# Expert row gathers issued as buffers free, the emptier expert moved to a y bank, rounded slot products: a decoder step with 64 experts on one NeuronCore

## The reference, cut to what matters

```python
def moe_ffn(h, lw):
    x = h.reshape(-1, h.shape[-1])                      # 1032 x 1024
    idx, wts = route(x, lw['router_w'], lw['router_bias'])   # 8 of 64 experts per token
    routed = routed_experts(x, idx, wts, lw['expert_w_gate'], lw['expert_w_up'], lw['expert_w_down'])
    shared = (silu(x @ lw['shared_w_gate']) * (x @ lw['shared_w_up'])) @ lw['shared_w_down']
    return routed + shared
# per expert e and the tokens that chose it (gate and up 1024 x 256, down 256 x 1024):
#   hb = silu(xb @ w_gate[e]) * (xb @ w_up[e]);  out[token] += (hb @ w_down[e]) * weight[token, e]
```

## Time and profile before

| what | before |
|---|---|
| median of three runs | 1831.04 us |
| the profiled execution: its time, and its span | 1831.6 us, 1829.8 us |
| PE / weight loads / DVE / ACT / GpSimd busy | 90% / 65% / 62% / 49% / 34% of the span |
| granted TensorE clock, mean | 0.953 of full |
| stages by time | to 748 us attention and mixing; 748 to 841 routing; 841 to 1752 experts; to 1830 the rest |
| share of DMA xg<-h_d,tokb in the chain that ended last | 22.0%, the largest |

### The profile page before, as it was taken

How to read it: one execution, slowest core, us unless ns; L and a number is a source line. 1 busy time by engine, 2 the same in 40 slices (tenths; PEclk the granted TensorE clock), 3 DMA queues, 4 the chain that set the end, 5 groups by cost and what they waited for, 6 DMA issues and landing times.

```text
span 1829.8 us, 26568 instructions
## 1 busy us (share of the span) xinstructions
PE 1643.9 (90%) x8857; PEld 1187.0 (65%) x8858; DVE 1129.6 (62%) x1575; ACT 904.9 (49%) x1389; POOL 626.5 (34%) x555
## 2 busy tenths in 40 slices
PE   4999999599998898687999999999999899999897
PEld 3555555333356667366888888878888787787743
DVE  2355575532235556666778777777787777777746
ACT  1011111232345454135777776776776676676633
POOL 0056676300000000113543554545455354454300
PEclk8999999689999999798999999999999999999999
DMA  9588866667761113646989889888898898988774
GB/s 349 195 279 274 273 207 216 246 205 217 238 226 63 65 52 152 255 156 244 311 287 316 294 300 319 277 301 304 281 328 283 295 312 279 329 278 299 267 240 187
DMA packets 156011, 457.45 MB, mean 250 GB/s; under 512 B 25375, under 2 KB 35806, under 8 KB 138458
## 3 DMA queue, kind: packets, MB, share of 16 engines
q1 hardware_dynamic: 119289, 368.12, 55.7%
q0 software_dynamic: 26624, 69.80, 14.7%
q10 hardware_dynamic: 9960, 17.83, 2.8%
HBM read 394.52 MB, written 78.15 MB: 258 GB/s over the span
## 4 chain that ended last, share of the span: by engine, by line
PE 28%; DMA 22%; issue 4%; ACT 2%; POOLq 1%; DVE 1%; POOL 1%; ACTq 0%; DVEq 0%
DMA xg<-h_d,tokb 22%; PE ps L2341 10%; PE ps L2360 6%; PE ps L2303 4%; PE ps L2694 2%; ACT yb L2266 2%; PE ps L2323 2%; PE ps L1840 1%; PE ps L1885 1%; PE ps L2712 1%; PE ps L2325 1%; PE ps L1856 1%; POOLq L2167 1%; POOL acc_d L2176 1%; PE ps L2328 0%
## 5 line engine op out<-in xcount | busy, mean ns | idle before, releaser
L2395 DVE TENSOR_TENSOR lo_gu<-raw_gu,hi_gu 128x1024 fp32r<-128x1024 f32 x256 | 301.5, 1219 | 14.5 <-ACT hi_gu L2216 13.1
L2176 POOL DMA_INDIRECT acc_d<-yb,tokb x96 | 175.6, 1829 | 344.5 <-ACT yb L2266 324.1
L2323 PE MATMUL ps<-xT_h,hi_gu 128*128 128x416 f32 (+4 forms) x896 | 266.1, 361 | 1.4 <-DVE gu_h L2409 1.4
L2216 ACT ACTIVATE hi_gu<-raw_gu 128x1024 fp32r<-128x1024 f32 x256 | 255.3, 1049 | 0.0
L602 PE MATMUL ps<-w_in_sb,hT 128*128 128x512 f32 x512 | 225.4, 598 | 1.1 <-ACT hT L466 1.1
L2325 PE MATMUL ps<-xT_h,lo_gu 128*128 128x208 f32 (+4 forms) x896 | 224.7, 251 | 0.0
L446 POOL TENSOR_TENSOR prod<-kring,qbc 128x512 f32<-128x512 f32 x128 | 159.5, 1274 | 177.6 <-DMA kring<-in_cache_k 122.2
L602 PEld LDWEIGHTS ps<-w_in_sb,hT 128*128 128x128 f32 x512 | 96.5, 191 | 118.7 <-issue 117.4
L2323 PEld LDWEIGHTS ps<-xT_h,hi_gu 128*128 128x128 f32 x896 | 169.1, 189 | 5.0 <-issue 2.4
L2325 PEld LDWEIGHTS ps<-xT_h,lo_gu 128*128 128x128 f32 x896 | 171.3, 191 | 1.2
L2360 PE MATMUL ps<-hi_dn,hT_h 128*128 128x512 f32 (+5 forms) x512 | 168.5, 400 | 0.0
(11 more groups left out here) (362 smaller groups left out, 2979.6 us busy)
## 6 DMA issues: line engine op xcount, KB each, us to landing
raw_gu<-in_expert_w_gate SPq DMA_DIRECT2D x64, 1024.0 KB, 9.9
raw_gu<-in_expert_w_up SPq DMA_DIRECT2D x64, 1024.0 KB, 13.5
raw_dn<-in_expert_w_down SPq DMA_DIRECT2D x64, 1024.0 KB, 10.0
kring<-in_cache_k SPq DMA_DIRECT2D x128, 256.0 KB, 3.1
vring<-in_cache_v SPq DMA_DIRECT2D x128, 256.0 KB, 3.0
adaw<-in_ada_w ACTq DMA_DIRECT2D x7, 2048.0 KB, 12.7
adaw<-in_ada_w SPq DMA_DIRECT2D x5, 2048.0 KB, 15.2
w_in_sb<-in_w_in SPq DMA_DIRECT2D x4, 2048.0 KB, 19.5
```

What stands on the lines that cost most here:

```text
L2176: pool.indirect_dma_start(out=acc_d[b % 2][:, :], out_offset=bass.IndirectOffsetOnAxis(ap=tokb[0:rows, b:b + 1], axis=0), in_=yb[b % 2][0: ...
L2216: act.activation(hi_cut(n, u), raw_cut(n, u), ACT.Copy).then_inc(hi_made, 1)
L2323: pe.matmul(ps[:, bank, 0:2 * cap], wh, x[:, k, :, :].rearrange("p a t -> p (a t)"), start=(k == 0), stop=False)
L2395: dve.tensor_tensor(lo_cut(n, u), raw_cut(n, u), hi_cut(n, u).bitcast(F32), ALU.subtract).then_inc(lo_made, 1)
```

## The change

Six things are done together.

1. GpSimd's order is written out by pair: gathers 0 to 3 ahead of the wait for the cleared accumulators, then scatter(3p-2), gather(3p+4), slot_weight(3p+2), scatter(3p-1), gather(3p+5), slot_weight(3p+3), gather(3p+6), slot_weight(3p+4), scatter(3p). The wslot ring grows from 4 to 6.
2. The light block's turn_x(3p+2) moves from the head of the pair into heavy ch 0, between its two halves; ACT and DVE handle it after the first three weight cuts instead of before them.
3. The light gate/up writes the first y bank of block 3p+1's parity (light_bank) instead of gate_bank. Its wait for sums_h 2p+2 becomes a wait for y_here 3p and moves, itself, to turn_h.
4. down(3p+1) writes that y bank next and gets a wait for hb_made p+1.
5. The slot products (L1885) take fp32r operands instead of fp32; they and ACT's numbered are spread between the steps of the shared expert, and turn_down(2) goes ahead of the last four.
6. The waits for y5_out go from GpSimd, ahead of gather(2), to ACT's first second_halves and DVE's rest_of_x(2).

```diff
         OH = 3
-        oh_p = [place(f"oh_p{j}", 160 + 4 * j, [P, TOPK, P]) for j in range(OH)]
-        oh_b = [place(f"oh_b{j}", 172 + 5 * j, [P, TOPK, NBLK]) for j in range(OH)]
+        oh_p = [place(f"oh_p{j}", 160 + 4 * j, [P, TOPK, P], F32R) for j in range(OH)]
+        oh_b = [place(f"oh_b{j}", 172 + 5 * j, [P, TOPK, NBLK], F32R) for j in range(OH)]
         y5 = [place(f"y5_{j}", dead + 4 * j, [P, D]) for j in range(2)]
...
                 act.wait_ge(oh_b_made, t + 1)
-                act.activation(oh_b[t % OH][:, :, :], oh_b[t % OH][:, :, :], ACT.Copy,
+                act.activation(oh_b[t % OH][:, :, :], oh_b[t % OH][:, :, :].bitcast(F32), ACT.Copy,
                                scale=c("ids")[:, t:t + 1]).then_inc(oh_b_ids, 1)
...
             evict(0)
+            numbered(0)
+            numbered(1)
             gated(2)
+            numbered(2)
             turned(1)
+            numbered(3)
+            numbered(4)
             evict(1)
-            for t in range(T9):
-                numbered(t)
+            numbered(5)
             turned(2)
+            numbered(6)
+            numbered(7)
             evict(2)
+            numbered(8)
             act.wait_ge(zeros_out, 16 * (2 * T9 - NWIN))
...
                 last.then_inc(dn5, 1)
...
+            def slots_of(t):
+                pe.wait_ge(oh_p_made, t + 1)
+                pe.wait_ge(oh_b_ids, t + 1)
+                for k in range(TOPK):
+                    last = pe.matmul(ps[:, 0, 0:NBLK], oh_p[t % OH][:, k, :], oh_b[t % OH][:, k, 0:NBLK],
+                                     start=(t == 0 and k == 0), stop=(t == T9 - 1 and k == TOPK - 1))
+                last.then_inc(tok_mm, 1)
 
...
             gate_up(2)
+            slots_of(0)
+            slots_of(1)
+            slots_of(2)
             turn_down(1)
-            for t in range(T9):
-                pe.wait_ge(oh_p_made, t + 1)
-                pe.wait_ge(oh_b_ids, t + 1)
-                for k in range(TOPK):
-                    last = pe.matmul(ps[:, 0, 0:NBLK], oh_p[t % OH][:, k, :], oh_b[t % OH][:, k, 0:NBLK],
-                                     start=(t == 0 and k == 0), stop=(t == T9 - 1 and k == TOPK - 1))
-                last.then_inc(tok_mm, 1)
+            slots_of(3)
+            slots_of(4)
+            turn_down(2)
+            for t in range(5, T9):
+                slots_of(t)
             pe.wait_ge(over_made, 1)
...
                       ).then_inc(over_mm, 1)
-            turn_down(2)
 
...
         wr = [place(f"wr{j}", 206 + 0.25 * j, [P, NE]) for j in range(4)]
-        wslot = [place(f"wslot{j}", 207 + j / 32, [P, 1]) for j in range(4)]
+        wslot = [place(f"wslot{j}", 207 + j / 32, [P, 1]) for j in range(6)]
         s_gu2 = place("s_gu2", 89, [P, 2, KC * F])
...
             return 2 + p % 2
...
+        def light_bank(p):
...
+            return 4 + 2 * ((3 * p + 1) % 2)
 
...
                 pool.wait_ge(wr_in[b % 4], 16 * (b // 4) + 16)
-                if b >= 4:
-                    pool.wait_ge(y_here, b - 3)
-                pool.tensor_copy(wslot[b % 4][:, :], wr[b % 4][:, bass.ds(e, 1)]).then_inc(wslot_here, 1)
+                if b >= 6:
+                    pool.wait_ge(y_here, b - 5)
+                pool.tensor_copy(wslot[b % 6][:, :], wr[b % 4][:, bass.ds(e, 1)]).then_inc(wslot_here, 1)
 
...
             pool.wait_ge(tok_ready, 1)
-            gather(0)
-            gather(1)
+            for b in range(4):
+                gather(b)
             pool.wait_ge(zeros_out, 16 * (2 * T9 - NWIN))
...
                 pool.wait_ge(y5_out[j], 16 * ((NWIN + 1 - j) // 2))
-            for b in range(MAIN):
-                if b + 2 < MAIN:
-                    gather(b + 2)
-                slot_weight(b)
-                if b >= 3:
-                    scatter(b - 3)
-            for b in range(MAIN - 3, MAIN):
-                scatter(b)
+            slot_weight(0)
+            slot_weight(1)
+            for p in range(PAIRS):
+                if p:
+                    scatter(3 * p - 2)
+                if p + 1 < PAIRS:
+                    gather(3 * p + 4)
+                slot_weight(3 * p + 2)
+                if p:
+                    scatter(3 * p - 1)
+                if p + 1 < PAIRS:
+                    gather(3 * p + 5)
+                    slot_weight(3 * p + 3)
+                    if p + 2 < PAIRS:
+                        gather(3 * p + 6)
+                    slot_weight(3 * p + 4)
+                scatter(3 * p)
+            scatter(MAIN - 2)
+            scatter(MAIN - 1)
             for j in range(2):
...
                     act.wait_ge(sums_h, t)
+                else:
+                    for j in range(2):
+                        act.wait_ge(y5_out[j], 16 * ((NWIN + 1 - j) // 2))
                 act.activation(half2[:, :, 0:cap], ps[:, 2:4, cap:2 * cap], ACT.Copy).then_inc(half2_here, 1)
...
                     act.wait_ge(hb_made, p)
-                act.activation(sg_l[:, :], ps[:, gate_bank(p), 0:F], ACT.Sigmoid).then_inc(sg_here, 1)
+                act.activation(sg_l[:, :], ps[:, light_bank(p), 0:F], ACT.Sigmoid).then_inc(sg_here, 1)
 
...
                 act.activation(yb[b % 2][0:rows, :], ps[0:rows, 4 + 2 * (b % 2):6 + 2 * (b % 2), :].rearrange("p b n -> p (b n)"),
-                               ACT.Copy, scale=wslot[b % 4][0:rows, 0:1]).then_inc(y_here, 1)
+                               ACT.Copy, scale=wslot[b % 6][0:rows, 0:1]).then_inc(y_here, 1)
 
...
             for p in range(PAIRS):
+                round_weights(cuts_at(p, HEAVY_FIRST))
                 round_x(3 * p + 2)
-                round_weights(cuts_at(p, HEAVY_FIRST))
                 second_halves(p, 0)
...
                 for h, bank in enumerate((gate_bank(p), 5 - gate_bank(p))):
+                    if h and ch == 0:
+                        turn_x(3 * p + 2)
                     if h and p and ch == 0:
...
                 pe.wait_ge(xT_made, 3 * p + 3)
-                pe.wait_ge(sums_h, 2 * p + 2)
+                if p:
+                    pe.wait_ge(y_here, 3 * p)
                 wh, wl = hi_gu[n % 2], lo_gu[n % RAWS]
...
                     for a, w in ((0, wh), (0, wl), (1, wh)):
-                        last = pe.matmul(ps[:, gate_bank(p), :].rearrange("p (a f) -> p a f", a=2), xT_l[a][:, k, :],
+                        last = pe.matmul(ps[:, light_bank(p), :].rearrange("p (a f) -> p a f", a=2), xT_l[a][:, k, :],
                                          w[:, :, k * F:(k + 1) * F], start=(k == 0 and a == 0 and w is wh),
...
                     pe.wait_ge(y_here, b - 1)
+                if b % 3 == 1:
+                    pe.wait_ge(hb_made, b // 3 + 1)
                 wh, wl = hi_dn[n % 2], lo_dn[n % RAWS]
...
                 pe.wait_ge(hb_made, p + 1)
+                pe.wait_ge(sums_h, 2 * p + 2)
                 for ch in range(FC):
...
             for p in range(PAIRS):
-                turn_x(3 * p + 2)
                 gate_up_heavy(p, 0)
...
             def rest_of_x(b):
+                if b == 2:
+                    for j in range(2):
+                        dve.wait_ge(y5_out[j], 16 * ((NWIN + 1 - j) // 2))
                 dve.wait_ge(xT_hi_made, b + 1)
...
             def gated_light(p):
-                bank = ps[:, gate_bank(p), :]
+                bank = ps[:, light_bank(p), :]
                 dve.wait_ge(sg_here, p + 1)
...
             for p in range(PAIRS):
+                rest_of_weights(cuts_at(p, HEAVY_FIRST))
                 rest_of_x(3 * p + 2)
-                rest_of_weights(cuts_at(p, HEAVY_FIRST))
                 add_halves(p, 0)
```

## The result

The changed kernel took 1743.51 us (median of four runs, 1739.92 to 1745.16) against 1832.90 us (1828.78 to 1839.86) before, a ratio of 0.952 with an interval of 0.949 to 0.955. It is faster by 89 us; 80 were forecast. The profiled execution took 1741.91 us, with a span of 1740.2.

The account below looks back on a forecast made before the run. The expert-stage loop, gather(3p+6) behind scatter(3p), with the sums wait over it, bounded the kernel at 28.38 us per pair. Gains of 61 (loop), 1 (pair 0), 3 (last pair), 15 (routing, start) gave 1751 us; range 1729 to 1788.

Parts of the forecast that it names:

- Two causes over each other: Before light gate/up, PE waits for x and for sums_h; the earlier gather alone would bring next to nothing.
- PE's work, 25.9 us per pair: Expert stage: PE's own work without waits, from about 26.8 us at 224 tokens to 25.0 at 160.
- The stall of 0.45 us per pair: Expert loop: PE stall allowed for late gathers, late scatter landings and fuller DMA, ends 0 and 1.5 us.
- The landing of the gathers: Gathers of x take 8.6 to 14.5 us to land, median 12.1; the tightest is late by up to 0.8.
- Moved turn at no cost: Light x turned mid-half in heavy ch 0: same 8 transposes, same 0.79 us, cost nil.
- The last pair's 2.83 us: In the last pair the wait of 2.83 us goes whole.
- Routing, 10 us: Routing stage: slot table done near 811 us instead of 821, 10 us gained (7 to 11.5).
- First heavy product, 5 us: Start of the expert stage: it needs only blocks 0 and 1, not the third x; 5 us more (3 to 6).
- the first rival, full cover: Expert loop: landings stay, PE never stalls, 25.9 us per pair, 1737 us; chance 0.15.
- The DMA engines as the next bound: Expert loop: gathers and scatters land 1 to 2 us later, pair 27.0 to 27.5 us, 1778 us; chance 0.25.
- The slower case, the closed loop through the scatter: scatter(3p) lands late, delaying eviction, hb, down(3p+1) and the next scatter; pair 30.2 us, 1867 us; chance 0.04.
- No gain in the loop: GpSimd's order or the ACT-DVE chain holds the pair at 28.4 us; 1813 us; chance 0.05.

Follow-up runs that it names:

- Gathers alone: Kernel before with only GpSimd's new order (parts 1 and 6: gathers, wslot ring of 6, y5_out waits): 1822.75 us, ratio 0.996.
- the run with gathers and bank: Kernel before with parts 1, 3, 4 and 6, without the moved turn or the routing: 1760.22 us, ratio 0.9603.
- The run with less PE work: Changed kernel without the third light gate/up product (rest of x times rounded weights): 1734.83 us, ratio 0.9484.
- late-gather kernel: Changed kernel with gather(3p+6) and slot_weight(3p+4) moved behind scatter(3p): 1792.97 us, ratio 0.9788.
- the routing alone: Kernel before with only part 5 (rounded slot products, spread between shared-expert steps): 1821.87 us, ratio 0.9947.
- the bank alone: Kernel before with only parts 3 and 4 (light gate/up in the y bank): 1810.16 us, ratio 0.9875.

## Why the prediction came out right

**Two causes over each other.** Right, and the main thing. Gathers alone left the pair at 28.34, together with the bank it is 26.36.

**PE's work, 25.9 us per pair, 26.8 to 25.0 by size.** Right: with 0.1 us of waits the pairs take 26.01, and 26.7 to 25.4; at 160 tokens 0.2 to 0.5 us of the 25.4 are the waits for hb, so 25.0 is right there too, as is the loss of some 0.2 us that I had put there.

**The stall of 0.45 us per pair.** This is the term that was mis-sized: it is 0.1. The size of the scatters' lateness was as said: ACT waited 11.3 us for them, 19 times, 0.6 us each, and the longest was 1.3. It is no more than before, when ACT waited 12.1 us, 22 times, in the same pairs. But down(3p+1) then waited for hb only 8 times, 2.9 us in all. I carried ACT's wait past a cover of 0.4 us to PE, at full size in every pair; 19 of some 31 had one at all. And I kept the spread of the landings up to 14.4 us, where acc_d now reaches 12.4. 0.35 us times 30 are the 10 us by which the loop did better than forecast (71 against 61). Inside the loop this is the first rival, full cover, and the forecast's own bounds of 0.2 to 0.8 did not hold it.

**The landing of the gathers.** I took 12.1 us in the median for every gather. It is 10.3, and most of the difference is in one of the three gathers of a pair, which the last section looks at. The Trainium skill (DMA: Bandwidth & Descriptors, Queues, rings and completion order) has the turns between queues, which I read as "the landing stays". The runs do not speak against the turns; my reading left out that a gather issued at another time meets other work, on its own queue and on SP's.

**Moved turn at no cost.** Right, and I left out what it brings: without it 0.3 us of the pair come back, most of them waits for x, as the tightest gathers have a half chain less.

**Scatter keeps its place, slot weights behind a waiting gather cost nothing.** Right: scatter(3p) is issued 1298.24 - 1293.25 = 5.0 us behind the first down product, as in the earlier trace rows (1347.83 - 1342.84).

**The last pair's 2.83 us.** It gained 3.95; the distance before also held a light product of 6.82 us instead of 5.3, 1.5 us of lower clock that I hadn't counted.

**Routing, 10 us.** 8.7 by the first gather. The table came 27.3 us after the first one-hot tile instead of 26.3, and most of that 1 us is DVE's: its last ring wait was 1.09 us (I had 1.5), but the fourth and the fifth t took 3.1 us each instead of 2.54, for a cause that the trace doesn't name. A t of products took 1.07 to 1.15 us instead of 1.03; the lower of the two prices was the right one.

**First heavy product, 5 us.** 4.1 (19.04 us behind the first gather before, 14.94 after; 3.6 in the run with gathers and bank). It begins right behind the second split of x, as foreseen. That it stands at 825.68, where I had said 826, is partly luck: 2.7 us came from the stages before.

**The rivals.** The DMA engines as the next bound (27.0 to 27.5 us per pair) is refuted: at a share of 0.96 and 321 GB/s they move the pair's 8.35 MB in 26.01 us and PE hardly waits. The slower case, the closed loop through the scatter, is a real loop, but it didn't make the pair slower: scatter(3p) landed in 11.1 us in the median, and PE's work covers the loop but for the waits for hb, most of them in the smaller pairs. The run with less PE work shows it right behind PE's work, at 26.0 us a round. No gain in the loop is what gathers alone would have been. One term of the range is misworded: its upper end, 1788 us, goes with a routing gain of 7 us instead of 10; with 7 us less it would be 1793.

In sum, against the profiled execution of 1741.9 us the forecast was 9 us too high: 10 too high for the stall, 1 for the last pair and 2.7 for stages that the change doesn't touch; 2.2 too low for routing and head and 1.7 for the first pair, and it had started 0.6 below the profiled execution of the kernel before. Against the median it was 7.5 too high.

## What to carry to other kernels

Where an engine waits twice in a row in each round, work out when it would be at the second wait if the first were gone; here either fix alone was worth 7 or 23 us and both 73. On an in-order queue that waits for its items, write the order by the time at which each item becomes free: one gather put ahead of one scatter held half of the gain. And before cutting work from the engine that bounds a loop, look for the loop without it: here it was just as long, so 1.8 us less work brought 0.13.

## What the runs showed of the hardware that I had not expected

**A gather lands sooner with no scatter just ahead of it and fewer weights under way.** Issue by issue in the stage, the 30 gathers of the changed kernel with no scatter in the 5 us before them landed in 7.4 us in the median (5.6 to 9.4), the 51 issued within 2.7 us of a scatter's start in 11.2 (6.2 to 13.1). In the kernel before only 4 were of the first kind (8.6 to 9.4), and the 37 close behind a scatter took 13.1. With the gathers alone the first kind took 5.0. In the late-gather kernel it is 12.8 for the 61 close ones. One of the first kind, the gather of the timeline above, issued at 1294.26, gave

```profile
DMA to landing us min/median/max: 8.7/8.7/8.7
```

against 12.86 for its like in the earlier trace rows.

Two things changed at once for these gathers, though. All 30 of the first kind are gather(3p+6), and while they were under way SP's queue, the weights, moved 161 GB/s in the mean (63 with the gathers alone); for the same gather it moved 251 in the kernel before and in the late-gather kernel. Within the changed kernel the two can be told apart a little: of the gathers in whose first 5 us SP's queue moved 180 to 230 GB/s, the 16 of the first kind took 8.3 us in the median and the 28 close behind a scatter 10.4, and the one close gather that met SP's queue at only 69 GB/s took 6.2. So at like weight traffic a scatter just ahead goes with some 2 us, and the weights count beside it. No run changed the one without the other.

**The clock.** In the kernel before 8 of the 32 light products lasted 6.3 to 6.9 us from first to last start, instead of 5.34; with gathers alone 8 did (one of them 8.1), with the routing alone 9 (from 6.0 on), with the bank alone 3, with the late gather 4, and in the kernels with pairs near 26 us none (the one with gathers and bank has one short stretch of lower clock elsewhere in a pair). One of them, in the kernel with gathers alone (stretches of 1065 to 1069 and 1069.2 to 1072 us, columns as in the earlier trace rows, and single products):

```profile
1065.00:1069.00 4.00, 2.30 (x18) 2.10 (x16) 3.15 (x4) 2.55 (x4) 2.51 (x2) 1.00 1.03 348
1069.20:1072.00 2.80, 2.80 (x9) 2.24 (x10) 2.30 (x5) 2.80 (x5) 1.53 (x3) 0.73 1.05 386
```
```profile
1069.96 0.39 PE L2355 MATMUL ps<-hi_gu,xT_lh 128*128 128x512 f32 x1
1070.19 0.39 PE L2355 MATMUL ps<-lo_gu,xT_lh 128*128 128x512 f32 x1
...
1071.60 0.63 PE L2355 MATMUL ps<-hi_gu,xT_ll 128*128 128x512 f32 x1
1072.03 0.63 PE L2355 MATMUL ps<-hi_gu,xT_lh 128*128 128x512 f32 x1
```

PE had stood 1.89 us ahead of this light product and was busy 2.30 of 4 us. Then, 1.2 us into it, the distance of two products goes from 0.23 to 0.43 us, the lower of the two clock levels (1.2 instead of 2.4 GHz), for some 3 us. It cost up to 1.6 us each time, some 12 us in all in the kernel before, 0.4 of its 28.37 us per pair. Mostly the pairs with the longest stalls pay: in the kernel before PE had stood 1.8 to 2.7 us in one piece ahead of each of the 8 slow light products, and ahead of the other 24 at most 1.75 us in 21 cases and 2.0 to 2.8 in three. The sum of the stalls alone doesn't settle it: with less PE work PE stood 42 us in the 30 pairs, in pieces of at most 1.8 us, and the granted clock stayed at 1.00. That the stalls brought the lower clock about is a reading, no run changed the one without the other, and which of the long stalls are followed by it stays open; with gathers alone 8 of the 24 pairs at full clock had one of 1.9 to 2.8 us too.
